# A relative-position bias table: one row per head in HBM, read with a forward skew and backwards on VectorE

## What is computed

```python
rel = np.clip(LEFT_CHUNKS * CHUNK + i_idx - j_idx, -(CHUNK - 1), REL_CLIP) + (CHUNK - 1)
bias = jnp.take(rel_bias, rel, axis=1)          # 16 heads; rel_bias is 16 x 192
sc = einsum('bhqd,bhkd->bhqk', q_blk, k[:, :, k0:k1]) * scale
sc = sc + bias[None, :, :, BAND - n_keys:]
p = softmax(sc, axis=-1)
```

## Time and profile before

| | |
|---|---|
| median of 3 runs | 982.45 us (979.15 to 982.84) |
| profiled execution, first to last instruction | 986.9 us |
| profiled execution, its own time | not recorded apart from its span |
| TensorE busy | 940.8 us, 95% of the span |
| VectorE, ScalarE, GpSimd busy | 558.4, 453.1, 37.1 us |
| mean granted clock of TensorE | 0.974 of full speed |
| moved by DMA | 156.85 MB, written to HBM 4.19 MB of it |

### The profile page before, as it was taken

One profiled execution on the slowest core, in us unless ns is written; L12 is line 12 of the kernel. 1 busy time (PEld: TensorE's weight loads), 2 busy tenths in 40 slices (PEclk: granted clock), 3 DMA queues, 4 the chain that ended last, 5 costly groups with the idle time before them and its releaser, 6 DMA issues.

```text
span 986.9 us, 14228 instructions
## 1 busy us (share of the span) xinstructions
PE 940.8 (95%) x5740; PEld 824.6 (84%) x5740; DVE 558.4 (57%) x718; ACT 453.1 (46%) x581; POOL 37.1 (4%) x83
## 2 busy tenths in 40 slices
PE   6999989599999998899999999999999999999997
PEld 6987778499999986767899999979886799999996
DVE  4695674355555555773755555565555555455553
ACT  5363444344444455573544444455445354343442
POOL 1000011000000012001100000010000010000000
PEclk9896999799999998999999999999999999999999
DMA  9352259855655443217456555556331526555541
GB/s 301 111 172 85 86 142 105 264 172 179 203 185 198 155 139 120 94 44 250 156 186 198 192 191 170 186 168 199 129 129 43 171 87 212 191 180 184 174 165 43
DMA packets 97671, 156.85 MB, mean 159 GB/s; under 512 B 4015, under 2 KB 72236, under 8 KB 97628
## 3 DMA queue, kind: packets, MB, share of 16 engines
q1 hardware_dynamic: 94908, 149.37, 46.3%
q0 software_dynamic: 1664, 6.82, 4.2%
q10 hardware_dynamic: 1056, 0.07, 0.1%
HBM read 152.06 MB, written 4.19 MB: 158 GB/s over the span
## 4 chain that ended last, share of the span: by engine, by line
PE 88%; DVE 4%; DMA 4%; ACT 2%; issue 1%; POOL 0%; DVEq 0%; ACTq 0%; SPq 0%
PE psum L1564 26%; PE psum L1565 26%; PE psum L1566 26%; DMA raw<-in_ffn_w 3%; PE psum L1977 2%; PE psum L1952 1%; PE psum L2010 1%; DVE h_lo L1048 1%; DVE w_lo L1023 1%; PE psum L1599 1%; PE psum L2030 1%; PE psum L1775 1%; PE psum L1744 1%; ACT w_hi L635 1%; ACT h_hi L662 1%
## 5 line engine op out<-in xcount | busy, mean ns | idle before, releaser
L1564 PE MATMUL psum<-h_hi,w_hi 128*128 128x256 f32 x1072 | 308.3, 288 | 19.6 <-DVE w_lo L1023 12.0
L1565 PE MATMUL psum<-h_lo,w_hi 128*128 128x256 f32 x1072 | 305.9, 285 | 0.0
L1566 PE MATMUL psum<-h_hi,w_lo 128*128 128x256 f32 x1072 | 305.7, 285 | 0.0
L1023 DVE TENSOR_TENSOR w_lo<-raw,w_hi 128x2048 fp32r<-128x2048 f32 (+2 forms) x74 | 164.0, 2222 | 127.5 <-ACT w_hi L635 127.2
L1564 PEld LDWEIGHTS psum<-h_hi,w_hi 128*128 128x128 f32 x1072 | 208.4, 194 | 24.6 <-DVE w_lo L1023 12.4
L1038 DVE TENSOR_TENSOR w_lo<-raw,w_hi 128x2048 fp32r<-128x2048 f32 x66 | 151.3, 2293 | 104.9 <-ACT w_hi L653 104.9
L1565 PEld LDWEIGHTS psum<-h_lo,w_hi 128*128 128x128 f32 x1072 | 208.6, 195 | 1.5
L1566 PEld LDWEIGHTS psum<-h_hi,w_lo 128*128 128x128 f32 x1072 | 208.3, 194 | 0.0
L635 ACT ACTIVATE w_hi<-raw 128x2048 fp32r<-128x2048 f32 (+2 forms) x74 | 136.0, 1842 | 103.3 <-PE psum L1566 85.2
L653 ACT ACTIVATE w_hi<-raw 128x2048 fp32r<-128x2048 f32 x66 | 126.0, 1908 | 69.5 <-PE psum L1566 69.5
L1564 PE MATMUL psum<-w_hi,g_hi 128*128 128x512 f32 x368 | 143.8, 391 | 0.0
(11 more groups left out here) (225 smaller groups left out, 823.9 us busy)
## 6 DMA issues: line engine op xcount, KB each, us to landing
raw<-in_ffn_w SPq DMA_DIRECT2D x64, 1024.0 KB, 5.2
raw<-in_ab_w_in SPq DMA_DIRECT2D x12, 1024.0 KB, 5.4
raw<-in_w_qkv SPq DMA_DIRECT2D x12, 1024.0 KB, 5.1
raw<-in_w_gate SPq DMA_DIRECT2D x11, 1024.0 KB, 5.3
raw<-in_w_up SPq DMA_DIRECT2D x11, 1024.0 KB, 5.4
raw<-in_w_down SPq DMA_DIRECT2D x11, 1024.0 KB, 4.9
raw<-in_ab_w_out SPq DMA_DIRECT2D x4, 1024.0 KB, 4.8
raw<-in_c_w_out SPq DMA_DIRECT2D x4, 1024.0 KB, 5.0
```

Source lines behind the costliest of these rows:

```text
L1023: ins = dve.tensor_tensor(dst, src, high, ALU.subtract)
L1564: pe.matmul(dst, stat[0], mov[0], start=first, stop=False)
L1565: pe.matmul(dst, stat[0], mov[1], start=False, stop=False)
L1566: return pe.matmul(dst, stat[1], mov[0], start=False, stop=last)
```

## The change

The scratch tensor holds each head's row once. The row is built the other way round: 64 copies of the first entry, the 191 following ones forwards, 129 copies of the last. The store has no broadcast (24 KB). The load starts partition p at element p of the one row, so all partitions read overlapping stretches of the same 16 rows. The tile then has its keys in falling order, so the masked columns are the first 64 and VectorE reads the bias with a step of -1.

```diff
-        rel_dram = nc.dram_tensor("rel_scratch", (H2, P, EXT), F32, kind="Internal")
+        rel_dram = nc.dram_tensor("rel_scratch", (H2, EXT), F32, kind="Internal")
...
-            pool.dma_start(rel_dram.ap(), rel_ext[:, :].unsqueeze(1).to_broadcast([H2, P, EXT])).then_inc(rel_stored, 16)
+            pool.dma_start(rel_dram.ap(), rel_ext[:, :]).then_inc(rel_stored, 16)
...
-                    pool.dma_start(bias2[:, :, :], bass.AP(rel_dram, P - 1, [[EXT - 1, P], [P * EXT, H2], [1, S]]))\
+                    pool.dma_start(bias2[:, :, :], bass.AP(rel_dram, 0, [[1, P], [EXT, H2], [1, S]]))\
                         .then_inc(bias_loaded, 16)
...
-                    pool.memset(bias2[0:CHUNK, :, P + CHUNK:S], NEG).then_inc(bias_ready, 1)
+                    pool.memset(bias2[0:CHUNK, :, 0:S - P - CHUNK], NEG).then_inc(bias_ready, 1)
...
-            n0 = P
+            n0 = S - N_REL
             n1 = n0 + N_REL - 1
-            step(dve.tensor_copy(rel_ext[:, 0:n0], rel_t[:, N_REL - 1:N_REL].to_broadcast([H2, n0])))
-            step(dve.tensor_copy(rel_ext[:, n0:n1], rel_t[:, N_REL - 2::-1]))
-            dve.tensor_copy(rel_ext[:, n1:EXT], rel_t[:, 0:1].to_broadcast([H2, EXT - n1])).then_inc(rel_built, 1)
+            step(dve.tensor_copy(rel_ext[:, 0:n0], rel_t[:, 0:1].to_broadcast([H2, n0])))
+            step(dve.tensor_copy(rel_ext[:, n0:n1], rel_t[:, 0:N_REL - 1]))
+            dve.tensor_copy(rel_ext[:, n1:EXT], rel_t[:, N_REL - 1:N_REL].to_broadcast([H2, EXT - n1]))\
+                .then_inc(rel_built, 1)
...
-                for qb, (c0, c1, k0) in enumerate(((0, P, P), (P, 3 * P, 0))):
+                for qb, (c0, c1, last) in enumerate(((0, P, P - 1), (P, 3 * P, S - 1))):
                     ins = dve.tensor_tensor_reduce(s2[:, h % 2, c0:c1], bank(2 + h % 2)[:, c0:c1],
-                                                   bias2[:, h, k0:S], -1.0, -NEG, ALU.add, ALU.min,
+                                                   bias2[:, h, last::-1], -1.0, -NEG, ALU.add, ALU.min,
                                                    nmax2[:, qb, h:h + 1])
```

## The result

The change made the kernel faster: 968.27 us median of 4 runs (967.04 to 978.35) against 981.98 us median of 4 runs of the kernel before, ratio 0.9871 with a 95% interval of 0.9827 to 0.9916. The unaltered kernel, run again (first experiment), gave 967.76 against 981.78: 14.0 us, ratio 0.9837 (0.9789 to 0.9884). The forecast was 968.1.

What follows compares the result with a forecast made beforehand. TensorE was taken as the bound, busy 940.8 of 986.9 us; 12.0 us of pause plus 2.4 us of low clock, all else 0, off the 982.45 median gave 968.05, stated as 968.1, range 964.5 to 974.5.

Steps and rivals of the forecast that it cites:

- The store, 12.0 + 2.4 us: In FFN0: shrinking the 3 MB store removes TensorE's 12.0 us wait for weights and 2.4 us of low clock.
- what is late next: nothing: In FFN0: no later weight load becomes the new wait, so the 14.4 us count in full.
- the starved load trails the store by 3.2 us: In FFN0: the delayed weight load lands 3.2 us after the store, at 181.4 against 178.15 us.
- Row building and masking, 0: The three row copies and POOL's masking of 64 x 1024 elements cost no time either way.
- The bias load, 0: The 2 MB load from 24 KB instead of 3 MB, around 451 us, changes the time by 0.
- my bounds of 5 and 23.5: Landing time of the 2 MB bias load: 5 us at the gain rows' rate, 23.5 us at the store's.
- 29 us: Beside FFN1: the bias load may land up to 29 us after issue before starved weights stop TensorE.
- The doubling to 19.5 us: Estimate by the skill page's ratio: bias load landing from 9.7 to 19.5 us, the sum still 14.4.
- VectorE backwards, 0: Third layer's attention: reading the bias backwards on VectorE costs 0, at most 2.5 us in the tail.
- Rival A: FFN0's pause is shorter in ordinary runs: gain 10 us, time 972.5; chance 0.22 including anything up to the main case.
- Rival B: Something other than the 3 MB store holds FFN0's weight load: time stays at 982; chance 0.05.
- rival C: The bias load crawls and starves FFN1's weights: at 46 us of landing, time 987.5; chance 0.04.

Runs made afterwards that it cites:

- first experiment: The changed kernel run again with no edit, beside more runs of the kernel before: 967.76 us against 981.78.
- 96 copies: Changed kernel plus an unread second store of the row 96 times over (2.25 MB): 974.02 us, ratio to before 0.9926.
- at 64: Changed kernel plus an unread second store of the row 64 times over (1.5 MB): 968.47 us, ratio to before 0.9869.
- at 256: Changed kernel plus an unread second store of the row 256 times over (6 MB): 1012.96 us, ratio to before 1.0327.

## Why the prediction was right

**The store, 12.0 + 2.4 us.** Right. FFN1 as the yardstick for FFN0 gave the gain of the two profiled executions to 0.02 us (14.42 predicted from the earlier trace rows, 14.40 found), and putting the store back alone took all of it away again. That closeness is in part luck: with the store put back FFN0 is 15.5 us longer than clean, 12.6 of pause and 2.9 of low clock. In the timed runs the gain is 13.7 us, and 14.0 in the larger set. The step "what is late next: nothing" held: FFN0 has no wait but the 1.1 us for its first input. The mechanism, a lead of fixed length, predicted the pause at 96 copies to 0.1 us and none at 64. One part of it was mis-sized: that the starved load trails the store by 3.2 us holds within 0.4 us at 96 and 128 copies, but at 256 it trails by nothing, and where the store was moved it lands 5 us ahead of it. One difference was misread: from 153.5, where the load lands without the store, to 169.4, where it has to be there, are 15.9 us and not 17; the sum doesn't use it.

**Row building and masking, 0.** Right by the kernel with the store put back, which contains both and is at 0.9989 of before.

**The bias load, 0.** Right in the sum; 9.9 us against the 9.7 of before and my bounds of 5 and 23.5. The gain of 3 us in landing that the broadcasts suggested did not come. The bound on it was wrong: "29 us" took over the starvation from the store, and beside this load, into 128 partitions, a weight load took 11.4 us at most with four of them. The doubling to 19.5 us that I estimated by the Trainium skill ("DMA: Bandwidth & Descriptors", section Latency and other measured facts) did not happen; reading the same 24 KB over and over took 9.9 us, reading out of 3 MB 9.7.

**VectorE backwards, 0.** Right, to 1 ns of 287 and 420, and within 0.2 us behind FFN1.

**Rival A** fell. The 4.45 us by which the profiled span lay above the median were not in the pause: that execution had lost 7.3 us at a low clock in the first layer, and the pause of the kernel with the store put back is 12.6 us in an execution that took 982.8 us, its median. **Rival B** fell with the store put back, **rival C** with the longer bias loads: its mechanism did not show for this transfer, even at six times the length.

## What to carry to other kernels

When a stage stands still on a load, look at what else the queues carried in that stretch, and at how many partitions it touches in SBUF: here a store out of 16 partitions took 2.6 times as long as the same bytes out of 128, and what was queued beside it starved. A background transfer costs what outlasts the lead of the loads that it starves, and the low clock behind that pause; the lead ends at the first engine that has the data in its list, not at the engine that needs it last. Where a kernel runs the same stage twice, the clean one prices the disturbed one better than any sum of parts.

## What the runs showed of the hardware that I had not expected

A 3 MB store took 35.0 us out of partitions 0 to 15, 19.0 out of 0 to 31, 18.9 out of 0 to 63 and 13.3 out of all 128. Beside the first, SyncE's queue got 4.2% of the engines' time (93.2% for the store), beside the last 13.4% (84.2%), beside bias loads into 128 partitions 46.6%. The low clock behind a pause cost FFN0 2.2 to 2.9 us, whether the pause was 3.7 or 42.8 us long. And the kernel's largest scatter has nothing to do with DMA: in a few executions TensorE, busy throughout, ran part of the first layer at a clock of 0.50, at a price of about 7 us in the profiled one of before.
